# Giving each stage's split operands their own byte distance from the split weights

## The reference, cut to what matters

```python
hl = modulate(rms_norm(xl, norm1_g[i]), mod_l[0], mod_l[1])
...                                     # conv_module or gqa_mixer
xl = xl + mod_l[5][:, None, :] * sq_relu_mlp(hl, w_ff1[i], w_ff2[i])
```

```python
h = swiglu(rms_norm_2(x, ng[0]), ffn_w_gate[l, 0], ffn_w_up[l, 0], ffn_w_down[l, 0])
x = x + 0.5 * rms_norm_2(h, ng[1])
...                                     # rwkv7 + retention, or sparse attention + short convolution
x = x + rms_norm_2(h, ng[3])
h = memory_xattn(rms_norm_2(x, ng[4]), mem_n, xa_wq[l], xa_wk[l], xa_wv[l], xa_wo[l])
...
h = swiglu(rms_norm_2(x, ng[6]), ffn_w_gate[l, 1], ffn_w_up[l, 1], ffn_w_down[l, 1])
```

## Time and profile before

| | |
|---|---|
| runs, median (lowest to highest) | 2259.95 us (2258.86 to 2261.04) |
| profiled execution, its own time | 2258.8 us |
| its span, first to last instruction | 2256.7 us |
| mean granted TensorE clock | 0.991 |
| TensorE matmul busy | 2165.3 us, 15970 matmuls |
| VectorE busy | 1498.3 us |
| ScalarE busy | 930.5 us |
| HBM traffic | 149 GB/s over the span |

### The profile page before, as it was taken

The page is one execution under the profiler, slowest core; times in us unless marked ns, Lnnn a source line. Parts: engine busy times, 40 slices in busy tenths (PEclk is TensorE's granted clock), DMA queues, the critical chain, the costliest instruction groups (busy, mean ns, idle before and its releaser), DMA issues.

```text
span 2256.7 us, 39544 instructions
## 1 busy us (share of the span) xinstructions
PE 2165.3 (96%) x15970; PEld 1893.9 (84%) x15970; DVE 1498.3 (66%) x2399; ACT 930.5 (41%) x1448; POOL 43.6 (2%) x37
## 2 busy tenths in 40 slices
PE   6999999999999999999999999999999999899997
PEld 3654678888778599999998987789989999688997
DVE  4779664444455866676667785476686677656666
ACT  3225532222233744454444452354454453345444
POOL 0000000000003000000001100000000000000000
PEclk9999999999999999999999998999999999999999
DMA  7768322232223045556554311355555554143553
GB/s 290 273 244 302 111 78 100 94 101 96 94 84 103 1 162 192 195 169 201 191 194 151 124 56 45 103 172 190 192 160 194 193 180 140 57 140 122 196 195 122
DMA packets 93556, 338.89 MB, mean 150 GB/s; under 512 B 10224, under 2 KB 12400, under 8 KB 93168
## 3 DMA queue, kind: packets, MB, share of 16 engines
q1 hardware_dynamic: 92096, 331.84, 43.9%
q10 hardware_dynamic: 1328, 5.21, 0.6%
HBM read 335.96 MB, written 1.05 MB: 149 GB/s over the span
## 4 chain that ended last, share of the span: by engine, by line
PE 85%; DVE 8%; ACT 4%; DMA 2%; issue 1%; SPq 0%; DVEq 0%; ACTq 0%
PE ps L556 21%; PE ps L558 21%; PE ps L557 21%; PE ps L963 2%; PE ps L661 2%; DMA ring<-weights 2%; PE ps L1234 1%; DVE WS L2058 1%; PE ps L579 1%; PE ps L920 1%; ACT HS L1827 1%; PE ps L910 1%; PE ps L1045 1%; PE ps L1068 1%; ACT WS L1514 1%
## 5 line engine op out<-in xcount | busy, mean ns | idle before, releaser
L2058 DVE TENSOR_TENSOR WS<-ring,WS 128x1024 fp32r<-128x1024 f32 x484 | 593.0, 1228 | 338.1 <-ACT WS L1514 337.2
L556 PE MATMUL ps<-HS,WS 128*128 128x256 f32 x2928 | 809.9, 277 | 6.6 <-DVE WS L2058 4.5
L558 PE MATMUL ps<-HS,WS 128*128 128x256 f32 x2928 | 806.0, 275 | 0.0
L557 PE MATMUL ps<-HS,WS 128*128 128x256 f32 x2888 | 794.7, 275 | 0.0
L1514 ACT CAST WS<-ring 128x1024 fp32r<-128x1024 f32 x484 | 506.7, 1049 | 550.8 <-PE ps L558 454.6
L556 PEld LDWEIGHTS ps<-HS,WS 128*128 128x128 f32 x2928 | 549.7, 188 | 10.3 <-DVE WS L2058 4.5
L558 PEld LDWEIGHTS ps<-HS,WS 128*128 128x128 f32 x2928 | 549.7, 188 | 0.0
L557 PEld LDWEIGHTS ps<-HS,WS 128*128 128x128 f32 x2888 | 542.2, 188 | 1.0 <-issue 1.0
L556 PE MATMUL ps<-CH,WS 128*128 128x512 f32 (+1 forms) x464 | 176.5, 380 | 0.3 <-DVE WS L2058 0.3
L557 PE MATMUL ps<-CH,WS 128*128 128x512 f32 (+1 forms) x464 | 173.9, 375 | 0.0
L558 PE MATMUL ps<-CH,WS 128*128 128x512 f32 (+1 forms) x464 | 173.8, 375 | 0.0
(11 more groups left out here) (418 smaller groups left out, 2686.3 us busy)
## 6 DMA issues: line engine op xcount, KB each, us to landing
ring<-weights SPq DMA_DIRECT2D x630, 512.0 KB, 3.6
X<-xs ACTq DMA_DIRECT2D x1, 2048.0 KB, 9.1
con<-const ACTq DMA_DIRECT2D x1, 2016.0 KB, 9.3
X<-mem ACTq DMA_DIRECT2D x1, 1024.0 KB, 5.5
y<-X SPq DMA_DIRECT2D x4, 256.0 KB, 2.2
vecs<-vec SPq DMA_DIRECT2D x1, 311.5 KB, 7.8
con<-const SPq DMA_DIRECT2D x1, 130.0 KB, 8.9
```

Source lines behind the costliest of these rows:

```text
L556: pe.matmul(dst, w[0][:, cut], upper, start=first, stop=False, skip_group_check=True)
L557: pe.matmul(dst, w[0][:, cut], lower, start=False, stop=False, skip_group_check=True)
L558: return pe.matmul(dst, w[1][:, cut], upper, start=False, stop=last, skip_group_check=True)
L2058: dve.tensor_tensor(WS[:, split % HALVES, 1, :], ring[:, panel % RING, :], WS[:, split % HALVES, 0, :].bitcast(F32), ALU.subtract).then_in ...
```

## The change

Only placement changes; no instruction, wait or transfer is added, removed or moved. HS2 and HTS get rooms of their own, each 128 values (512 bytes) larger than the data; so do HID and CH. A stage takes its view of a room at its own offset, in values of 4 bytes:

```diff
-        split = sb("HS2", 28 + 2 * KT * T + 4 * T + 108, dt=F32R)
-        HS2 = split[:, 28:28 + 2 * KT * T].rearrange("p (a k t) -> p a k t", a=2, k=KT)
-        HTS = split[:, 28 + 2 * KT * T:28 + 2 * KT * T + 4 * T].rearrange("p (b a t) -> p b a t", a=2, b=2)
+        hs_room = sb("HS2", 2 * KT * T + 128, dt=F32R)
+        hts_room = sb("HTS", 2 * 2 * T + 128, dt=F32R)
+        sb("con_pad", 8)
...
-            HID = convolution.enter_context(nc.sbuf_tensor("HID", [P, 11, 2, 2 * T], F32R))
-            CH = convolution.enter_context(nc.sbuf_tensor("CH", [P, 2, KT, 2 * T], F32R))
+            hid_room = convolution.enter_context(nc.sbuf_tensor("HID", [P, 11 * 4 * T + 128], F32R))
+            ch_room = convolution.enter_context(nc.sbuf_tensor("CH", [P, 4 * KT * T + 128], F32R))
...
+        HS_AT = {"wo": 4, "mlp1": 36, "f0": 40, "m0": 44, "f1": 52, "f2": 56, "m1": 26, "f3": 50}
+        HTS_AT = {"mlp1": 46, "f0": 30, "f1": 26, "f2": 44, "f3": 36, "m1": 0}
+        CH_AT = {"conv": 0, "pw1": 20, "pw2": 4, "mlp0": 40, "gqa": 48}
+        STAGE = {"wo": "wo", "rt": "m0", "rw": "m0", "ds": "m1", "sc": "m1"}
+        def hs2(tag):
+            return hs_room[:, HS_AT[tag]:HS_AT[tag] + 2 * KT * T].rearrange("p (a k t) -> p a k t", a=2, k=KT)
+        def hts(tag):
+            return hts_room[:, HTS_AT[tag]:HTS_AT[tag] + 4 * T].rearrange("p (a b t) -> p a b t", a=2, b=2)
+        def chs(tag):
+            return ch_room[:, CH_AT[tag]:CH_AT[tag] + 4 * KT * T].rearrange("p (a k t) -> p a k t", a=2, k=KT)
+        HID = hid_room[:, 28:28 + 44 * T].rearrange("p (n a t) -> p n a t", n=11, a=2)
...
-        SCP = area(19456, KT, 32)
+        SCP = area(19712, KT, 32)
-        RELU, RELU2 = area(19456, 2, 2 * T), area(20480, 2, 2 * T)
+        RELU, RELU2 = area(19712, 2, 2 * T), area(20736, 2, 2 * T)
-        MSQ = area(19456, KT, T)
+        MSQ = area(19712, KT, T)
-        stored = HID[:, :, :, :].rearrange("p a b c -> p (a b c)")
-        YU = HS2[:, 1, :, :]
+        stored = hid_room[:, 0:44 * T]
+        YU = hs2("m1")[:, 1, :, :]
```

More of the change, by code:

```diff
@@ L558, in three_products, with first_two @@
                 return pe.matmul(dst, w[1][:, cut], upper, start=False, stop=last, skip_group_check=True)
-            def first_two(dsts, starts, tag, halves=lambda half, k: HS2[:, half, k, :], sums=False):
+            def first_two(dsts, starts, tag, halves=None, sums=False):
+                halves = halves or (lambda half, k: hs2(tag)[:, half, k, :])
                 ws = split_panel(), split_panel()
@@ L587, in split_section, with split_tile @@
                 sections.append((panels[0], size))
-            def split_tile(dst, name, first=True, halves=lambda half, k: HS2[:, half, k, :]):
+            def split_tile(dst, name, first=True, halves=None):
+                halves = halves or (lambda half, k: hs2(STAGE[name[:2]])[:, half, k, :])
                 w = split_panel()
@@ L818, in queries @@
                 for q in range(2):
-                    split_tile(ps[:, KQ_BANK[u], q * T:(q + 1) * T], f"kq{u}", q == 0, lambda half, k: CH[:, half, k, LAT])
+                    split_tile(ps[:, KQ_BANK[u], q * T:(q + 1) * T], f"kq{u}", q == 0, lambda half, k: chs("gqa")[:, half, k, LAT])
                     if u == KEYS and q == 0:
@@ L829, in value_rows @@
                     for t in range(4):
-                        x = [CH[:, half, k, t * P:(t + 1) * P] for half in range(2)]
+                        x = [chs("gqa")[:, half, k, t * P:(t + 1) * P] for half in range(2)]
                         dst = ps[:, 4 + t // 2, (t % 2) * T:(t % 2 + 1) * T]
@@ L1025, in split_rows @@
                     for t in range(2):
-                        x = [HS2[:, half, k, t * P:(t + 1) * P] for half in range(2)]
+                        x = [hs2("m0")[:, half, k, t * P:(t + 1) * P] for half in range(2)]
                         dst = ps[:, bank + t, :]
@@ L1599, in _ @@
                     part = slice(g * T, (g + 1) * T)
-                    s.step(act.activation(CH[:, 0, k, part], H[:, k, part], ACT.Identity, bias=MOD[:, k, g:g + 1],
+                    s.step(act.activation(chs("pw1")[:, 0, k, part], H[:, k, part], ACT.Identity, bias=MOD[:, k, g:g + 1],
                                           scale=GS[:, 0, k, g:g + 1]).then_inc(act_done, 1), f"pw1_u{k}")
@@ L1649, in _ @@
                 act.wait_ge(act_done, s.n)
-                s.step(act.copy(CH[:, 0, k, :], H[:, k, :]).then_inc(act_done, 1), f"pw2_u{k}")
+                s.step(act.copy(chs("pw2")[:, 0, k, :], H[:, k, :]).then_inc(act_done, 1), f"pw2_u{k}")
             act.activation(small[:, 1:2], eps6, ACT.Sqrt)
@@ L1667, in _ @@
                     act.wait_ge(dve_done, at("dve", f"n1g{k}_{g}"))
-                    s.step(act.activation(CH[:, 0, k, part], H[:, k, part], ACT.Identity, bias=mlp_shift(0, g)(k)).then_inc(act_done, 1),
+                    s.step(act.activation(chs("mlp0")[:, 0, k, part], H[:, k, part], ACT.Identity, bias=mlp_shift(0, g)(k)).then_inc(act_done, 1),
                            f"mlp0_u{k}")
@@ L1693, in _ @@
                     act.wait_ge(dve_done, at("dve", f"n2g{k}_{g}"))
-                    s.step(act.activation(CH[:, 0, k, part], H[:, k, part], ACT.Identity, bias=MOD[:, 48 + k, g:g + 1]).then_inc(act_done, 1),
+                    s.step(act.activation(chs("gqa")[:, 0, k, part], H[:, k, part], ACT.Identity, bias=MOD[:, 48 + k, g:g + 1]).then_inc(act_done, 1),
                            f"gqa_u{k}")
@@ L1826, in pre_norm @@
                     act.wait_ge(*after(*wait(k)))
-                    s.step(act.activation(HS2[:, 0, k, :], XL(k), ACT.Identity, scale=gain(k)).then_inc(act_done, 1), f"{tag}_u{k}")
+                    s.step(act.activation(hs2(tag)[:, 0, k, :], XL(k), ACT.Identity, scale=gain(k)).then_inc(act_done, 1), f"{tag}_u{k}")
                     if k % 2:
@@ L2201, in _ @@
                 dve.wait_ge(dve_done, s.n)
-                s.step(dve.tensor_tensor(CH[:, 1, k, :], CV[:, k, :], CH[:, 0, k, :].bitcast(F32), ALU.subtract).then_inc(dve_done, 1),
+                s.step(dve.tensor_tensor(chs("pw1")[:, 1, k, :], CV[:, k, :], chs("pw1")[:, 0, k, :].bitcast(F32), ALU.subtract).then_inc(dve_done, 1),
                        f"pw1_l{k}")
@@ L2272, in _ @@
                 dve.wait_ge(act_done, at("act", f"pw2_u{k}"))
-                s.step(dve.tensor_tensor(CH[:, 1, k, :], H[:, k, :], CH[:, 0, k, :].bitcast(F32),
+                s.step(dve.tensor_tensor(chs("pw2")[:, 1, k, :], H[:, k, :], chs("pw2")[:, 0, k, :].bitcast(F32),
                                          ALU.subtract).then_inc(dve_done, 1), f"pw2_l{k}")
@@ L2479, in lower_inputs @@
                     dve.wait_ge(act_done, at("act", f"{tag}_u{k}"))
-                    s.step(dve.scalar_tensor_tensor(out=HS2[:, 1, k, :], in0=X[:, k, LAT], scalar=gain(k),
-                                                    in1=HS2[:, 0, k, :].bitcast(F32), op0=ALU.mult,
+                    s.step(dve.scalar_tensor_tensor(out=hs2(tag)[:, 1, k, :], in0=X[:, k, LAT], scalar=gain(k),
+                                                    in1=hs2(tag)[:, 0, k, :].bitcast(F32), op0=ALU.mult,
                                                     op1=ALU.subtract).then_inc(dve_done, 1), f"{tag}_l{k}")
```

52 lines of the change are left out of this document (26 added, 26 removed).

## The result

The changed kernel's median is **2320.52 us** (2320.02 to 2321.01) against 2259.95 us: a ratio of **1.0259, 95% interval 1.0239 to 1.028**. The prediction was 2274 us, in a range up to 2306, with 0.89 on "within 2%". It was wrong; the time came out next to its rival "112 is a narrow good place" (2324 us).

The account below looks back on a forecast made before the run. The prediction took TensorE's matmul spacing as the bound. Terms of +14.3 (f1 to f3 inputs), +0.8 (wo) and -0.6 (gqa) gave +14.5 us on 2258.8, or 2273.3, stated as a median of 2274 us; range 2251 to 2306.

Parts of the forecast that it names:

- 112 is a narrow good place: Split matmuls: everything further than 8 bytes from 112 pays 6.7 ns per 256-column matmul, +50.7 us, 2324 us in all; chance 0.14.
- What bounds the kernel: Split products from HS2 on: TensorE does not wait, so the spacing of its matmuls sets the end; 96% busy.
- The nearest-row rule on a line from 0 to 256: 256-column matmuls: each new distance takes the spacing seen at the nearest of 0, 112 and 256; borders 56 and 184.
- 104 to 184: row 112, no change: mlp1, f0, m0, m1 and hidden tiles of f1, f2, f3: spacing stays at 113.3 ns, no cost.
- the term of 14.3 us for 208, 224 and 200: Input panels of f1, f2, f3: 3168 matmuls, each 4.5 ns slower, +14.3 us.
- 512 columns, no change: pw1, pw2 and mlp0, 2112 matmuls leaving distance 0: no change, with ends of +14.4 and -23.2 us.
- split_rows' 233.3: 512-column matmuls with WS moving and HS2 standing still at 112: 233.3 ns, held a poorer witness than a moving CH.
- wo and gqa: wo at 16 slows by 0.8 us; gqa's latent queries and value rows at 192 gain 0.6 us.
- Wrong in kind if a tile's own address counts: Stated sign of error: spacing set by a tile's own address, not by where two streams stand to each other; no size.
- Distance is not the cause: Split matmuls: only exact multiples of 256 cost, or distance does not matter; time 2258 to 2260 us; chance 0.27.
- Room below: Conflict in the 226.5 ns avoided: mlp0, pw1, pw2 gain up to 23.2 us, others less; 2230 us; chance 0.13.

Follow-up runs that it names:

- the map: Kernel before with WS, CH and HID unchanged, but a different distance from WS for each stage's use of HS2 and HTS: 2300.5 us.

## Why the prediction was wrong, point by point

- *What bounds the kernel: right.* All but the 6.5 us of taps and recurrence was spacing; no wait of TensorE grew, and no other engine mattered.
- *The nearest-row rule on a line from 0 to 256: wrong, and the step that failed.* "104 to 184: row 112, no change" was measured at 117.5 to 122.2 ns in mlp1, f0, m0, m1 and the hidden tiles. f1 to f3 are 25.8 us longer; about 9.1 of this is their hidden tiles (22 panels x 24 x (120.1 + 119.0 + 118.7 - 3 x 113.5) ns), the rest, 16.6, their inputs. So the term of 14.3 us for 208, 224 and 200 was nearly right, by luck and not by its rule: they paid what the places called free paid too. With mlp1, f0, m0 and m1 (22.0) the rule missed 31 us.
- *The rule had no ground in the rows.* Its three points were two, as 0 and 256 are one place, and no row showed that the spacing is smooth between them. It is not: 4 bytes from 112 cost as much as 112 bytes. What the rows did say was a count, which I gave to the rival and did not weigh: of four steady rows at other distances than 112, three lay up.
- *512 columns, no change: wrong, inside its stated ends.* 7.8 us of the 14.4 that the upper end allowed: CH at 160 had 234.3 ns, HID at 112 231.2 in three quarters. I had called split_rows' 233.3 a poorer witness; what made it so stays open. Its stationary operand HS2 stood at 112, 16 bytes off a 32-byte place, but with HS2 at 64, on such a place, split_rows had 233.3 too (the map and the run with 64 everywhere).
- *wo and gqa: right in sign,* 0.46 for 0.8 and -0.53 for -0.6, not by the rule: wo at 16 had 118.7 ns, not row 0's 120.0, and gqa's queries ran partly at 113.3, its key tiles with 512 columns slower than before.
- *"Narrow good place": the nearest to what the runs showed.* It priced 7560 matmuls at 6.7 ns, 50.7 us, and spared all within 8 bytes of 112. In fact those paid too, 9000 matmuls (mlp1 1536, f0 to f3 4 x 1584, m0 624, m1 384, wo 120), 48.2 us in all, 5.4 ns each. Its 512 columns were 7 us too dear; the 6.5 us of taps and recurrence made up for that, so part of its nearness is luck. I gave it 0.14 and took a quarter of it into the range, which is why the range missed.
- *"Wrong in kind if a tile's own address counts": half.* The weights' place counts by 32 bytes, and the distance counts as well. The change left WS alone, so its whole cost came by the distance.
- *"Distance is not the cause" and "Room below": fallen;* 113.3 and 226.5 ns stayed the lowest. The Trainium skill (SBUF - State Buffer, Who interferes with whom) has the moving operand's read port and that of the weight loads independent. The runs do not bear out that a place therefore does not matter: 113.3 to 122.2 ns by distance alone.

What stays open: why it is so. The steady spacings seen most, 113.3, 120.0, 226.7 and 233.3 ns, are 17, 18, 34 and 35 times 6.67 ns, which is 16 cycles at 2.4 GHz, as if the streams met in steps of that size; but 116.7 stood as steadily (17.5 times), others (118.4, 119.1) are means of a repeating pattern, and no run shows what the streams wait for. Nor did a run show what picks the state.

## What to carry to other kernels

Where matmuls follow each other with a fresh weight load each, read the spacing from start times, by stage, before moving a buffer: in this kernel the byte distance of the moving operand from the weights, modulo 256, was worth up to 5% of a stage (f3: 9.2 of 177 us) while TensorE's busy share stayed at 96% and it waited no longer. Keep the weights on a 32-byte place, hold one measured distance for each width of matmul, and treat every distance not yet seen as unknown, not as its neighbour's. A place should also be judged by whether the stream returns to the lower spacing after a pause.

## What the hardware showed that I had not expected

- Two steady states at one place: 113.3 and 117.8 ns at 64 bytes, held for some 170 us and changed at a pause; 226.5 and 231.2 at 112 with 512 columns, changed without one.
- A shift of all operands by 16 bytes costs 49 us, one by 32 nothing.
- 112 is right for 256 columns and not for 512: there 0 had 226.7 ns throughout mlp0.
- Eleven runs of one kernel lay between 2249.53 us, with a mean granted clock of 0.996, and 2263.53, with 0.987. So single runs are read here by their spacings, and by their times only from some 15 us up.
